# Reordering the weight splits, sums and side units of two gated FFN stages in a one-core block kernel

## What is computed

```python
def swiglu(x, w_in, w_out):
    gate, up = jnp.split(x @ w_in, 2, axis=-1)
    return (jax.nn.silu(gate) * up) @ w_out

h = h + 0.5 * swiglu(rmsnorm(h, ffn1_norm[l]), ffn1_w_in[l], ffn1_w_out[l])
...                      # gMLP group, stick-breaking attention, cross-attention
h = h + 0.5 * swiglu(rmsnorm(h, ffn2_norm[l]), ffn2_w_in[l], ffn2_w_out[l])
```

## Time and profile before

| | us |
|---|---|
| median of 3 runs | 2141.73 |
| lowest, highest | 2141.57, 2141.74 |
| profiled execution, its own time | 2143.15 |
| its span, first to last instruction | 2141.4 |

### The profile page before, as it was taken

The page is one execution under the profiler, slowest core; times in us unless marked ns, Lnnn a source line. Parts: engine busy times, 40 slices in busy tenths (PEclk is TensorE's granted clock), DMA queues, the critical chain, the costliest instruction groups (busy, mean ns, idle before and its releaser), DMA issues.

```text
span 2141.4 us, 26534 instructions
## 1 busy us (share of the span) xinstructions
PE 2091.0 (98%) x9297; PEld 1720.2 (80%) x9297; DVE 1684.6 (79%) x1919; ACT 1195.6 (56%) x1373; POOL 79.7 (4%) x98
## 2 busy tenths in 40 slices
PE   9999899999999999999999999999997999999998
PEld 7888677778888888888888888887886777778887
DVE  8999788889998676566565656669997888889986
ACT  7555566645555565456544555555555656645554
POOL 0000000000000030000000000000000000000000
PEclk9999999999999999999999999999998999999999
DMA  8776988878876877875598766677778887879664
GB/s 289 224 235 215 274 239 251 265 221 253 250 241 213 269 255 215 241 216 183 177 284 240 233 206 188 206 220 222 214 227 234 270 259 235 243 248 274 206 208 157
DMA packets 192246, 497.75 MB, mean 232 GB/s; under 512 B 17824, under 2 KB 68384, under 8 KB 192032
## 3 DMA queue, kind: packets, MB, share of 16 engines
q1 hardware_dynamic: 183088, 464.11, 68.1%
q0 software_dynamic: 8640, 31.99, 7.7%
q10 hardware_dynamic: 432, 0.53, 0.1%
HBM read 468.77 MB, written 27.79 MB: 232 GB/s over the span
## 4 chain that ended last, share of the span: by engine, by line
PE 72%; DVE 13%; issue 7%; ACT 4%; DMA 3%; DVEq 0%; SPq 0%; ACTq 0%; POOL 0%; POOLq 0%
PE acc L2351 10%; PE acc L2353 10%; PE acc L2354 10%; DVE w_lo L1468 5%; PE acc L2457 5%; PE acc L2458 5%; PE acc L2459 5%; PE acc L2376 4%; PE acc L2374 4%; PE acc L2375 4%; DMA raw<-in_ffn_w_in 3%; ACT w_hi L907 3%; PE aux L2374 1%; PE aux L2375 1%; PE aux L2376 1%
## 5 line engine op out<-in xcount | busy, mean ns | idle before, releaser
L1468 DVE TENSOR_TENSOR w_lo<-raw,w_hi 128x1024 fp32r<-128x1024 f32 x717 | 866.0, 1223 | 349.5 <-ACT w_hi L907 348.6
L907 ACT ACTIVATE w_hi<-raw 128x1024 fp32r<-128x1024 f32 x717 | 743.1, 1055 | 675.0 <-PE acc L2354 273.4
L2351 PE MATMUL acc<-w_hi,a_hi 128*128 128x512 f32 x616 | 239.9, 389 | 0.0
L2353 PE MATMUL acc<-w_lo,a_hi 128*128 128x512 f32 x616 | 239.7, 389 | 0.0
L2354 PE MATMUL acc<-w_hi,a_lo 128*128 128x512 f32 x616 | 239.7, 389 | 0.0
L2351 PE MATMUL acc<-w_hi,b_hi 128*128 128x512 f32 x448 | 175.6, 392 | 0.0
L2353 PE MATMUL acc<-w_lo,b_hi 128*128 128x512 f32 x448 | 174.4, 389 | 0.0
L2354 PE MATMUL acc<-w_hi,b_lo 128*128 128x512 f32 x448 | 174.4, 389 | 0.0
L2457 PE MATMUL acc<-w_hi,hid_hi 128*128 128x512 f32 x432 | 168.3, 390 | 1.5 <-DVE w_lo L1468 1.5
L2458 PE MATMUL acc<-w_lo,hid_hi 128*128 128x512 f32 x432 | 168.1, 389 | 0.0
L2459 PE MATMUL acc<-w_hi,hid_lo 128*128 128x512 f32 x432 | 168.1, 389 | 0.0
(11 more groups left out here) (400 smaller groups left out, 3708.6 us busy)
## 6 DMA issues: line engine op xcount, KB each, us to landing
raw<-in_ffn_w_in SPq DMA_DIRECT2D x301, 512.0 KB, 4.5
raw<-in_ffn_w_out SPq DMA_DIRECT2D x176, 512.0 KB, 4.3
raw<-in_w_mix_in SPq DMA_DIRECT2D x80, 512.0 KB, 4.6
raw<-in_w_ckv SPq DMA_DIRECT2D x64, 512.0 KB, 4.3
memq<-bounce SPq DMA_DIRECT2D x196, 128.0 KB, 4.5
side_raw<-in_ffn_w_in SPq DMA_DIRECT2D x48, 512.0 KB, 6.5
side_lo<-in_ffn_w_in POOLq DMA_DIRECT2D x48, 512.0 KB, 8.2
bounce<-stage SPq DMA_DIRECT2D x35, 512.0 KB, 5.4
```

Source lines behind the costliest of these rows:

```text
L907: eng.activation(w_hi[:, u % RING], raw[:, u % RING], ACT.Copy).then_inc(w_hi_done, 1)
L1468: eng.tensor_tensor(w_lo[:, u % RING], raw[:, u % RING], w_hi[:, u % RING].bitcast(f32), ALU.subtract).then_inc(w_lo_done, 1)
L2351: eng.matmul(dst, x_hi[:, rows], w_hi[:, slot, i], start=start and i == 0, stop=False)
L2353: eng.matmul(dst, x_hi[:, rows], w_lo[:, slot, i], start=False, stop=False)
```

## The change

1. **Side units 0 and 1 of pair 5.** SP loads them ahead of the loop over the early pairs. ACT's last early pair (j = 4) is taken out of its loop, and side unit 0 is split behind the second plain unit after fast group 0, side unit 1 behind that after fast group 1.
2. **Fast group 0 of each pair from pair 1 on.** ACT: split first unit, sums' high parts, split second unit (before: both units, then the sums). DVE: rest of first unit, rest of the sums, rest of the second unit.
3. **End of a late pair.** ACT splits plain units 8 and 9 ahead of the side unit of group 3, unit 10 behind it, and unit 11 ahead of SiLU (before: behind it). DVE makes the rest of unit 10 ahead of the first addition of the gate half, and that of unit 11 ahead of the writes to `stage` (before: behind the last subtraction).
4. **`hidden`** of a late pair goes from behind group 1 to behind group 2, and the send that waits for it from ring unit 8 to ring unit 10.
5. **Pair 0.** The third group of squares moves from step 15 to step 13 (first stage). In the second stage the mixed blocks of group 3 are made first (step 7), those of groups 0, 1, 2 at steps 9, 11, 13 (before: 0 to 3 at 7, 9, 11, 13).

The diff, cut to its core:

```diff
-LATE_SEND_AT = 8
+LATE_SEND_AT = 10
...
-H3_MIX_AT = [7, 9, 11, 13]
-X_SQUARES_AT = [10, 11, 15, 15]
+H3_MIX_AT = [9, 11, 13, 7]
+X_SQUARES_AT = [10, 11, 13, 15]
...
@@ sync
+                if base != FFN1_IN:
+                    eng.wait_ge(w_used, base)
                 load_side(DC + 1, 0, base != FFN1_IN)
                 load_side(DC + 1, 1, base != FFN1_IN)
+                with eng.Fori(1, DC + 1) as j:
...                              (the loop over the early pairs' loads, before: ahead of load_side)
@@ scalar, fast_hi of an early pair
                     split(base, j, p, PAIR)
-                    split(base, j, p + 1, PAIR)
+                    if s:
+                        split(base, j, p + 1, PAIR)
                     sums_hi(s, fast_count(base, j, s))
+                    if s == 0:
+                        split(base, j, p + 1, PAIR)
...
                         split(base, j, FAST_AT[s] + 3, PAIR)
+                        if s < sides:
+                            side_split_of(DC + 1, s)
@@ scalar, late_pair
                         late_split(j, LATE_FAST_AT[s])
-                        late_split(j, LATE_FAST_AT[s] + 1)
+                        if s:
+                            late_split(j, LATE_FAST_AT[s] + 1)
                         sums_hi(s, late_count(base, j, s))
+                        if s == 0:
+                            late_split(j, LATE_FAST_AT[s] + 1)
+                        if s == MIXES - 1:
+                            late_split(j, LATE_END)
+                            late_split(j, LATE_END + 1)
                         if s < 2:
                             side_split_of(j, 2 + s)
...
-                    late_split(j, LATE_END)
+                    late_split(j, LATE_END + 2)
                     eng.wait_ge(w_used, late_unit(base, j) + LATE_END)
                     eng.activation(copy_p1, sum_p1, ACT.Copy).then_inc(p1_copied, 1)
-                    late_split(j, LATE_END + 1)
-                    late_split(j, LATE_END + 2)
+                    late_split(j, LATE_END + 3)
                     eng.wait_ge(gate_added, fast_pairs[base] + j)
...                              (SiLU)
-                    late_split(j, LATE_END + 3)
...
-                with eng.Fori(1, DC + 1) as j:
+                with eng.Fori(1, DC) as j:
                     pair(j, first_hi[:, bass.ds(4 * j - 4, 4), :])
-                side_split_of(DC + 1, 0)
-                side_split_of(DC + 1, 1)
+                pair(DC, first_hi[:, 4 * DC - 4:4 * DC, :], sides=2)
@@ vector, late_pair (an early pair has the same change for s == 0)
                         late_lo(p)
-                        late_lo(p + 1)
+                        if s:
+                            late_lo(p + 1)
                         sums_lo(count)
                         if s == 0:
+                            late_lo(p + 1)
+                        if s == 0:
                             up_drained(j - 1, late_unit(base, j))
-                        if s == 1:
+                        if s == 2:
                             hidden(j - 1, 0)
                             hidden(j - 1, 1)
                     late_lo(LATE_END)
                     late_lo(LATE_END + 1)
+                    late_lo(LATE_END + 2)
...                              (shared[:, 0], shared[:, 1])
-                    late_lo(LATE_END + 2)
+                    late_lo(LATE_END + 3)
...                              (stage, shared)
-                    late_lo(LATE_END + 3)
```

More of the change, by code:

```diff
@@ L681, in late_pair @@
                         load(w, PAIR * j + p, late_unit(base, j), p)
+                if base != FFN1_IN:
+                    eng.wait_ge(w_used, base)
                 load_side(DC + 1, 0, base != FFN1_IN)
                 load_side(DC + 1, 1, base != FFN1_IN)
+                with eng.Fori(1, DC + 1) as j:
+                    for p in range(PAIR):
+                        if p == SEND_AT:
+                            send(number(TURNS, hid) - 1 + j, stage[:], hid_done, silus[base] + j)
+                        if p == FETCH_AT:
+                            fetch(number(TURNS, hid) - 1 + j, first=base == FFN1_IN)
+                        load(w, PAIR * j + p, base + PAIR * j, p)
                 with eng.Fori(DC + 1, FJ - 1) as j:
@@ L968, in to_stage, with mix_parts_hi @@
                 last.then_inc(staged, 1)
-            def mix_parts_hi(base, s, hi, used):
-                eng.wait_ge(mix_ready, MIXES * (fast_pairs[base] > 0) + s + 1)
+            def mix_parts_hi(base, n, s, hi, used):
+                eng.wait_ge(mix_ready, MIXES * (fast_pairs[base] > 0) + n + 1)
                 if s == FAST:
@@ L1010, in fast_hi, with pair @@
                     split(base, j, p, PAIR)
-                    split(base, j, p + 1, PAIR)
+                    if s:
+                        split(base, j, p + 1, PAIR)
                     sums_hi(s, fast_count(base, j, s))
-                def pair(j, hid_dst):
+                    if s == 0:
+                        split(base, j, p + 1, PAIR)
+                def pair(j, hid_dst, sides=0):
                     for s in range(FAST):
@@ L1552, in mix_parts, with mix_parts_lo @@
                 eng.tensor_tensor(parts[:, 3], parts[:, 2], whole[:, 2], ALU.add).then_inc(ready, 1)
-            def mix_parts_lo(base, s, hi, lo):
-                eng.wait_ge(mix_hi_done, MIXES * (fast_pairs[base] > 0) + s + 1)
+            def mix_parts_lo(base, n, s, hi, lo):
+                eng.wait_ge(mix_hi_done, MIXES * (fast_pairs[base] > 0) + n + 1)
                 parts = stage4[:, 2:4].rearrange("p a (b n) -> p (a b) n", b=2)
@@ L1656, in pair @@
                         unit_lo(j, p)
-                        unit_lo(j, p + 1)
+                        if s:
+                            unit_lo(j, p + 1)
                         sums_lo(count)
+                        if s == 0:
+                            unit_lo(j, p + 1)
                         unit_lo(j, FAST_AT[s] + 2)
```

9 lines of the change are left out of this document (4 added, 5 removed).

## The result

The changed kernel takes 2092.8 us (median of 4 runs, 2092.07 to 2093.54) against 2141.73 us (4 runs, 2141.57 to 2145.36): ratio 0.9768, 95% interval 0.9751 to 0.9785. That is 48.9 us less, where 52.7 were forecast; the time lies in the range. The profiled execution's span is 2090.4 us, 51.0 less than before.

What follows compares the result with a forecast made beforehand. PE, busy 98% of the span, was taken as the bound, so only its gaps could be regained: 24.8 + 25.7 + 0 + 2.3 + 1 = 53.8 us off 2141.7, plus 1 us for small gaps, gives 2089 us; range 2083 to 2103.

Steps and rivals of the forecast that it cites:

- step (pairs 4 and 5): Step from early to late pairs: PE's stand and low clock go, 11.8 us in the first stage, 13.0 in the second.
- pairs 6 to 10: Late pairs of both stages: the 2.64 us lost at each start goes, about 2.3 in the last; 25.7 us together.
- the term of pair 0: PE's waits at its first pair behind pair 0: 0.3 us back in first stage, 2.0 in second; bounds 1 and 4.
- pairs 2 and 3 (early pairs): New order in early pairs' group 0: value 0, bounds -1.5 (0.2 us in each of 8 pairs) and +1.3.
- behind the stages (output products): PE's `w_lo` waits in the output products, 1.5 us in all: 1 us gained through DVE's lead, bounds 0 and 3.
- 0.5 us of slack pays for 0.4: Early pairs, group 1: the sums' 0.5 us of slack absorbs about 0.4 us that DVE idles in group 0.
- fewer than five waits for `t_lo_part`: Sign of being right: PE waits for the sums' rest fewer than five times, at group 1 if anywhere.
- DMA as the bound: Rival: DMA engines set the late pairs; half the gain there gives 2102 us (chance 0.08), none 2115 (0.03).
- The early pairs on DVE: Rival: early pairs turn to DVE, eight pairs lose up to 0.6 us each, 2094 us; chance 0.09.
- The slower case: Late pairs: send at ring unit 10 holds SP's queue beyond T + 28; to T + 33 costs 54 us; chance 0.02.

Runs made afterwards that it cites:

- Parts 3 and 4 alone: Kernel before with only the late pairs' earlier splits and rests, and the later `hidden` and send: 2112.40 us, ratio 0.9851.
- part 1 alone: Kernel before with only side units 0 and 1 of pair 5 loaded ahead of the early pairs and split in pair 4: 2120.97 us, ratio 0.9893.
- without part 5: Changed kernel with the old order of squares and mixed blocks in pair 0 put back: 2096.33 us, ratio to before 0.9788.

## Why the prediction was right, and where it was not

The terms of the sum beside what PE's rows give for them, in us for the two stages together (rounded, so the last digit of the sum can differ):

| term | forecast | measured |
|---|---|---|
| step (pairs 4 and 5) | 24.8 | 23.4 |
| pairs 6 to 10 | 25.7 | 25.1 |
| pair 1 (the term of pair 0) | 2.3 | 2.3 |
| pairs 2 and 3 (early pairs) | 0 | -1.5 |
| behind the stages (output products) | 1 | 3.2 |
| ahead of pair 1, first stage | none | -1.4 |
| sum | 53.8 | 51.0 |

The two large terms are right by their mechanism. The small ones are not, and that the sum comes so near owes something to luck: 2.2 us more behind the stages than forecast cover the early pairs.

**The step to the late pairs: right.** SP's queue behind the side splits was the cause: without the early splits the stand is back, with them alone it is gone. The clock never fell once PE did not stand. What was mis-sized is what is left: 0.6 us at group 1 of pair 5 was forecast in each stage, and pair 5 is 1.3 and 1.1 us above its 40.80. I had taken DVE's lag from the trace before; with the side units in pair 4 the ring loads land later (ACT waits up to 3.07 us for one), which I had weighed only for pair 5's own loads.

**The late pairs: right.** Forecast 40.8 us for a pair; measured 40.80, with no wait. Parts 3 and 4 alone do it. DVE's lead at a pair's start was over 3 us by my count, and with it the order of group 0 makes no difference there. Whether part 4 is needed, I had not priced; it is worth nothing that one run can tell.

**The early pairs: wrong.** Forecast 0 with bounds -1.5 and +1.3; putting the old order back gives 4.7 us, and pair 2 of the first stage alone lost 1.3. Against the kernel before, pairs 2 and 3 show only 1.5 of it. There the two of the second stage took 42.2 us each, but 41.5 with part 1 alone and with parts 3 and 4 alone, neither of which changes them; the cause stays open. The step that failed is "0.5 us of slack pays for 0.4". The 0.4 was right (0.36 measured), but I followed only DVE and ACT. The rest of the second unit also frees a ring slot, and with it SP's next load; that came 2 us later, and cost DVE another 0.55 us before the next sums. SP's queue, which waits for that `w_lo`, was the one that I had left out of the sum. I had asked for fewer than five waits for `t_lo_part` as a sign of being right: there are eight, at group 1 of six of the eight early pairs and of both pairs 5, and none in pairs 6 to 10.

**Pair 0 and the output products.** Pair 1 gained 0.7 and 1.6 us in the two stages where 0.3 and 2.0 were forecast, and without part 5 it is 0.9 and 2.2 us longer. No wait is left before its first product. The waits for `w_lo` in the output products (1.5 us in all) are gone; the stretches behind the stages give 3.2 us, just above the bound of 3. With parts 3 and 4 alone they give 2.4, so most of it is DVE's lead from the late pairs' tail.

**The rivals.** DMA as the bound is refuted for this load: 1 MB more read and 1 MB more written in each late pair changed nothing, and slices of about 1 us there ran at up to 430 GB/s, above the 358 that the prediction names. The early pairs on DVE, which I had priced at 5 us with a chance of 0.09, is the one that came true: its 2094 is nearer to the measured 2092.8 than my 2089. The slower case, SP held at the send, did not arise: the send goes at 320.03, 16.2 us behind the pair's start (303.81), where 16 were counted.

## What to carry to other kernels

In a kernel that is bound by one engine, count that engine's instructions in each stretch and look for the queue behind which its supply stands: here one wait in the loads' queue cost 9 to 11 us twice, and the low clock behind it 2 to 3 us more. Moving work earlier where an engine idles cost that engine nothing here, but its transfers came along: with both side units in pair 4 the ring loads landed 1.1 us later. Moving one step ahead of another has a price, if the second frees a buffer, since every load behind that buffer moves with it. When several edits go in together, take each out alone: one of five here cost 5 us and was covered by the rest.

## What the runs showed of the hardware

The first microseconds differ between executions of like code. PE in the profiled executions of before and after, in the same place of pair 0 (start, length of a row; `x2` is two matmuls):

```profile
9.00 0.62 PE L2584 MATMUL acc<-w_hi,a_lo 128*128 128x512 f32 x2
```

```profile
8.97 1.06 PE L2600 MATMUL acc<-w_hi,a_lo 128*128 128x512 f32 x2
```

Two matmuls take 0.62 us here and 1.06 there, and the number that PE starts from 4 to 12 us differs in the same way:

```profile
4.00:12.00 8.00, 7.07 (x32) 5.44 (x32) 5.91 (x11) 6.17 (x12) 0.00 (x0) 1.00 1.01 362
```

```profile
4.00:12.00 8.00, 7.43 (x24) 5.90 (x23) 5.92 (x11) 6.43 (x13) 0.00 (x0) 1.00 1.01 361
```

32 against 24 (and 34 in the kernel without part 5, 23 and 22 in two others), though the clock column says 1.00 in all. Rows of this length, 0.43 us apart, are what PE shows behind the stand, where the granted clock was 0.54. So the start looks like the low level (1.2 GHz) lasting some 4 us longer in the second execution; the column does not confirm it. Ten starts fewer at 0.23 us each are 2.3 us, an estimate. Each kernel has one profile, so that executions of one and the same kernel differ like this is not shown; it may be part of the spread of their times, and a difference of 2 us between two kernels' single profiles should not be read without looking there.
